# Second block: queries, keys and values ahead of the convolution inputs, and the convolution's taps spread further back

## The reference

```
xn = rms_norm(x, norm1_g)
proj = xn @ w_in + b_in                 # 2048 conv columns, 1024 q, 128 k, 128 v
conv: a * sigmoid(gate), causal depthwise convolution over 31 tokens on 1024 channels,
      + bias, layer_norm over the channels, silu
attention: rms norm of q and k heads, partial rotary, window of 128, sinks, softmax, values
x = x + concat(conv_out, attn_out) @ w_out
x = x + peer(rms_norm(x, norm2_g))      # keys, top-k, 16384 experts computed densely
```

## Time and profile before

| | us |
|---|---|
| median of 3 runs | 3307.56 (3307.48 to 3308.05) |
| the profiled execution's own time | 3305.67 |
| its span, first to last instruction | 3303.9 |
| PE busy | 3249.3 (98%) |
| PEld busy | 2823.9 (85%) |
| DVE busy | 2296.0 (69%) |
| ACT busy | 1546.5 (47%) |
| chain of waits: PE, DVE, ACT | 89%, 9%, 2% |
| mean granted TensorE clock | 0.995 |

### The profile page before, as it was taken

The page is one execution under the profiler, slowest core; times in us unless marked ns, Lnnn a source line. Parts: engine busy times, 40 slices in busy tenths (PEclk is TensorE's granted clock), DMA queues, the critical chain, the costliest instruction groups (busy, mean ns, idle before and its releaser), DMA issues.

```text
span 3303.9 us, 47459 instructions
## 1 busy us (share of the span) xinstructions
PE 3249.3 (98%) x19858; PEld 2823.9 (85%) x19858; DVE 2296.0 (69%) x3281; ACT 1546.5 (47%) x1975; POOL 9.9 (0%) x22
## 2 busy tenths in 40 slices
PE   9999999999999999998999999999999999999999
PEld 7998888888888888887789999888888888888887
DVE  6765556677577577798669987578787577865554
ACT  4554444555455355455544444444343444435353
POOL 0000000000000000000000000000000000000000
PEclk9999999999999999999999999999999999999999
DMA  7546666656655655552455554655656565565665
GB/s 239 162 150 213 216 207 180 210 188 189 190 191 184 198 186 172 185 163 69 158 160 167 170 169 135 196 168 156 183 173 191 186 184 180 182 185 188 192 189 166
DMA packets 163095, 592.25 MB, mean 179 GB/s; under 512 B 18112, under 2 KB 18272, under 8 KB 161984
## 3 DMA queue, kind: packets, MB, share of 16 engines
q1 hardware_dynamic: 161424, 583.15, 56.3%
q0 software_dynamic: 1456, 6.06, 0.6%
HBM read 587.04 MB, written 2.10 MB: 178 GB/s over the span
## 4 chain that ended last, share of the span: by engine, by line
PE 89%; DVE 9%; ACT 2%; issue 1%; DMA 0%; SPq 0%; DVEq 0%; ACTq 0%
PE PS L1063 19%; PE PS L1083 15%; PE PS L1085 14%; PE PS L1084 14%; PE PS L1066 10%; PE PS L1093 4%; PE PS L1094 4%; PE PS L1095 4%; DVE LO L1582 3%; PE PS L1260 1%; DVE GB L1996 1%; PE PS L1273 1%; ACT HI L1282 1%; PE PS L1117 0%; ACT UN L1358 0%
## 5 line engine op out<-in xcount | busy, mean ns | idle before, releaser
L1582 DVE TENSOR_TENSOR LO<-RAW,HI 128x1024 fp32r<-128x1024 f32 x1096 | 1327.0, 1218 | 731.9 <-ACT HI L1282 728.7
L1282 ACT ACTIVATE HI<-RAW 128x1024 fp32r<-128x1024 f32 x1096 | 1149.7, 1054 | 1149.9 <-PE PS L1085 722.1
L1063 PE MATMUL PS<-XX,HI 128*128 128x512 f32 x2688 | 735.5, 395 | 0.0
L1083 PE MATMUL PS<-HI,FH 128*128 128x512 f32 x1760 | 694.4, 395 | 5.7 <-DVE FL L1582 5.4
L1085 PE MATMUL PS<-HI,FL 128*128 128x512 f32 x1760 | 686.8, 390 | 0.0
L1084 PE MATMUL PS<-LO,FH 128*128 128x512 f32 x1760 | 685.3, 389 | 0.0
L1063 PEld LDWEIGHTS PS<-XX,HI 128*128 128x128 f32 x2688 | 459.6, 189 | 61.9
L1093 PE MATMUL PS<-XX,HI 128*128 128x256 f32 x1664 | 479.1, 288 | 9.8 <-DVE LO L1582 9.5
L1094 PE MATMUL PS<-XX,HI 128*128 128x256 f32 x1664 | 471.2, 283 | 0.0
L1095 PE MATMUL PS<-XX,LO 128*128 128x256 f32 x1664 | 471.0, 283 | 0.0
L1066 PEld LDWEIGHTS PS<-XX,LO 128*128 128x128 f32 x2688 | 412.4, 189 | 57.2
(11 more groups left out here) (280 smaller groups left out, 2090.7 us busy)
## 6 DMA issues: line engine op xcount, KB each, us to landing
RAW<-in_peer_v SPq DMA_DIRECT2D x256, 512.0 KB, 4.0
RAW<-in_ffn_w_up SPq DMA_DIRECT2D x176, 512.0 KB, 4.2
RAW<-in_peer_ut_rest SPq DMA_DIRECT2D x160, 512.0 KB, 3.6
RAW<-in_w_in SPq DMA_DIRECT2D x136, 512.0 KB, 4.2
RAW<-in_peer_ut SPq DMA_DIRECT2D x96, 512.0 KB, 3.6
RAW<-in_ffn_w_down SPq DMA_DIRECT2D x88, 512.0 KB, 3.9
RAW<-in_w_mix_out SPq DMA_DIRECT2D x32, 512.0 KB, 3.8
RAW<-in_w_in_2c SPq DMA_DIRECT2D x32, 512.0 KB, 3.6
```

Source lines behind the costliest of these rows:

```text
L1063: e.matmul(o, hi[:, k, x], XX[:, 4 * u + k, :, :].rearrange("p h s -> p (h s)"), start=first and k == 0, stop=False, skip_group_check=True)
L1083: e.matmul(o, x, hi[:, k, :], start=first and k == 0, stop=False, skip_group_check=True)
L1282: return e.activation(dst, src, ACT.Copy) if scale is None else e.activation(dst, src, ACT.Copy, scale=scale)
L1582: return e.tensor_tensor(dst, src, hi.bitcast(F32), ALU.subtract)
```

## The change

The order of the second block's list is rewritten. `q2,0` to `q2,2` come first, with 16 diagonals beside them and no taps. Beside `h2,0` go the heads' norms and 14 empty background advances; attention follows them at rate 1.5, beside `h2,1` to `h2,3`, with two taps for each unit. The loop without weight units now ends when attention and the second set of diagonals are through (its background rate is still 2), and no longer waits for TensorE's conv blocks or the taps. `o2` carries what the taps' generators give, one advance a unit; behind it a loop runs until taps and TensorE's conv blocks are done, and only then `layer_normed` is appended and flushed, before `o2_last`. Blocks 4 and 5 take three taps for each advance. R2 and RD2 move into the first block's mask, and the wait on `h2,3` before the copy of attention's output goes. The weight units' list follows the new order of products. The numbers of instructions on each engine stay the same.

```diff
@@ plan: the order of weight units
-    units("w_in_2c", [0, 1])
     units("w_in_2q", [0, 1])
     units("w_in_2kv", [0], 256)
-    units("w_in_2c", [2, 3])
+    units("w_in_2c", range(4))
@@ plan: the second block
-    conv_input(0)
-    beside.append(causal([0, 1], 3))
-    conv_input(1)
-    beside.append(causal([2, 3], 3))
     background.append(build(range(16)))
     for g in range(3):
         product(("q2", g), 8)
@@
-    beside.insert(0, together(heads_normed(0), heads_normed(1)))
+    beside.append(together(heads_normed(0), heads_normed(1)))
+    background.append(pause(14))
+    background.append(attention(2, (1, 2)))
     background.append(build(range(16, 31)))
-    background.append(attention(2, (1, 2)))
+    rate[0] = 1.5
+    conv_input(0)
+    beside.append(causal([0, 1], 2))
+    conv_input(1)
+    beside.append(causal([2, 3], 2))
     conv_input(2)
-    beside.append(causal([4, 5], 4))
+    beside.append(causal([4, 5], 3))
     conv_input(3)
     on_pe = [causal_pe((6, 7))]
     rate[0] = 2
-    while on_pe or (2, 1) not in done:
+    while background or (2, 1) not in done:
         step()
         advance(on_pe)
-    while beside:
-        advance(beside)
     rate[0] = 1
@@
-    background.append(layer_normed())
     for g in range(4):
         product(("o2", g), 4)
         emit("o2", g)
+    while on_pe or beside:
+        advance(beside)
+        advance(on_pe)
+    background.append(layer_normed())
     flush()
@@ buffers
-    R2, RD2 = STAGE[:, 8, :], STAGE[:, 9, :].rearrange("p (t s) -> p t s", t=2)
+    R2, RD2 = const("mask1")[:, 0:256], const("mask1")[:, 256:512].rearrange("p (t s) -> p t s", t=2)
@@ scalar: att_value
                 if a_ == 2:
                     w.wait_ge(s_mm, multiplied(LAST_DOWN))
-                    w.wait_ge(s_dve, V("h2", 3, k=2))
```

## The result

The changed kernel took 3335.26 us (median of 4 runs, 3334.06 to 3336.43) against 3307.52 (3306.58 to 3308.05) beside it: a ratio of 1.0086, 95% interval 1.0073 to 1.0099. Slower by 27.7 us, where 17.2 were forecast. The time lies above the band that the forecast itself was given (3317 to 3332, with a chance of 0.62) and inside the wider range (3311 to 3338), near its upper end.

The account below looks back on a forecast made before the run. TensorE, busy 98% of the span, was taken to bound the kernel. The steps summed to 292.6 us against 275.2, less 0.2 for a shorter first unit: +17.2 on 3307.56, about 3325 us, range 3311 to 3338.

Parts of the forecast that it names:

- q2: Queries, keys and values first, with diagonals and no taps beside them: bound by TensorE, 52.7 us.
- four conv inputs: Units h2,0 to h2,3 with heads' norm and attention beside them: 108.7 us, bounds 106.2 and 120.
- left before o2: Stretch without weight units ahead of o2, with 10 attention steps and 18 taps: 31.5 us, bounds 23.3 and 36.
- o2: 16 weight units with two taps each, the LayerNorm's matmuls no longer in it: 43.5 us.
- behind o2: Weight units stopped while 88 taps and 27 conv matmuls are left: 36.5 us, bounds 29 to 38.
- LayerNorm, with its share of slow clock: Bare LayerNorm chain between the taps and o2_last: 16.1 us, plus 2.0 for slow mean and variance matmuls.
- slow clock at o2_last: TensorE's reduced clock at o2_last's start, after idleness: 1.6 us.
- Heads' norm and attention beside the conv inputs: Norm beside h2,0: 9.7 us of stalls and slow clock become 0.6; attention beside h2,1 to h2,3: 1.4 of stalls.
- in-order rival: Attention beside conv inputs starves the divisions: 120 us there, 36 before o2, 3341 in all; chance 0.18.
- The charge for the clock: TensorE's slow clock after idleness: 2.0 us at mean and variance matmuls, 1.6 at o2_last's start.
- Cheap by itself: Work standing alone runs at its own rate: attention rest 18.9 us, a tap 0.31, total 3299; chance 0.07.
- The wash: Rest before o2 takes only TensorE's 23.3 us, no stall before it: 3315, or 3311 with cheaper taps; chance 0.13.

Follow-up runs that it names:

- e6_diag: Changed kernel with diagonals 16 to 30 built ahead of attention, which also begins one advance earlier: 3333.15 us, 1.0079 to the kernel before.
- e3_out_last: Changed kernel with VectorE's copy of TensorE's conv block 7 queued behind all taps: 3331.11 us, 1.0077 to the kernel before.
- e2_back: Kernel before with only the back half of the change, the loops around o2 and the bare LayerNorm: 3319.11 us, 1.0040 to the kernel before.
- e4_warm: Changed kernel with idle filler matmuls on TensorE beside the last taps and in the LayerNorm: 3334.28 us, 1.0086 to the kernel before.
- v2_spread: Kernel before, attention two advances later, rate 2 beside h2,3; remaining taps and conv blocks under o2's start, LayerNorm under its last two groups: 3311.94 us, 1.0018.
- v6: Kernel before with one conv input ahead of q2, attention beside the last three; last taps, then LayerNorm under o2: 3307.75 us, 1.0002.
- v7: As v6, but all taps finished before o2 and the LayerNorm beside o2 from its start: 3305.08 us, 0.9995 to the kernel before.
- e5_three: Changed kernel with three taps instead of two for each advance in blocks 0 to 3: 3321.08 us, 1.0046 to the kernel before.

## Why the prediction was right or wrong

Right in sign and mechanism (taps and LayerNorm left bare), too small by 10.5 us: the time missed the forecast's own band of 3317 to 3332 and stayed inside the range because that left room for stalls. By its steps, forecast and measured in us:

| step | forecast | measured |
|---|---|---|
| q2 | 52.7 | 54.0 |
| four conv inputs | 108.7 | 109.2 |
| left before o2 | 31.5 | 36.2 |
| o2 | 43.5 | 43.8 |
| behind o2 | 36.5 | 41.2 |
| LayerNorm, with its share of slow clock | 18.1 | 19.2 |
| slow clock at o2_last | 1.6 | 2.6 |
| sum | 292.6 | 306.2 |

The last row is 0.06 of 43.5 us, from that window's clock of 0.94; by the starts of its first matmuls it is 2.4. The 275.2 of before taken off leaves +31.0; the stretch before was cut 0.4 us short, as o2_last began at 1633.9. The rest of the profile is within a microsecond of what it was, and the difference of spans is 30.2. The medians differ by 27.7. q2's excess of 1.3 was not looked into beyond one wait of 0.8 us for an operand of the spread.

*Heads' norm and attention beside the conv inputs.* Right: no wait of 5 us before the transposes, VectorE at 87%, and 109.2 us where the in-order rival wanted 120.

*What is left before o2: the first step that was mis-sized, by 4.7.* The forecast counted from the list of steps, by which attention has passed the third exp of its second query block when the units end, and so it put one exp and three divisions into the stretch. The engines were behind the list. ScalarE's timeline in the changed kernel, the first part of each of the four exps (each four parts of 0.49 us), the first division and the first diagonals:
```profile
1519.00 0.49 ACT L1360 ACTIVATE UN<-UN,SM 128x256 f32<-128x256 f32 x1
...
1521.92 0.49 ACT L1360 ACTIVATE UN<-UN,SM 128x256 f32<-128x256 f32 x1
...
1524.83 1.69 ACT L1284 ACTIVATE UN<-UN,SM 128x256 f32<-128x256 f32 x4
...
1526.43 0.49 ACT L1360 ACTIVATE UN<-UN,SM 128x256 f32<-128x256 f32 x1
...
1534.10 0.51 ACT L1360 ACTIVATE UN<-UN,SM 128x256 f32<-128x256 f32 x1
...
1541.95 1.27 ACT L1284 ACTIVATE UF<-CONST,PAR 128x128 f32<-128x128 f32 x4
```
When the units ended at 1521.4, one exp was done; three exps and all four divisions lay in the stretch. TensorE waited 5.1 us for the first division, a term that the forecast didn't have, and then 2.9 for h2,3's output, where it had 4: together 4.0 more, most of the 4.7. The diagonals were too dear in the forecast, not too cheap: by the list 8 stand before the last values and not 12. That the backlog makes the excess is read from this trace; e6_diag, which happens to start attention one advance earlier, moves the wait to h2,3's output and saves 1 to 2 us, and no run removes the backlog itself.

*Behind o2: the second, again by 4.7.* The taps were counted right (88 at 0.397 = 34.9), but I gave conv block 7's copy its own 0.4 us and not its wait. I had written that 12 us of conv matmuls go "with" the taps; the copy sits among the taps in an in-order queue. e3_out_last took 4.9 us off the tail, and 3 to 4 off the timed runs, by moving that one instruction.

*LayerNorm and clock.* Right to 1.1 and 1.0 us. e2_back gives the bare LayerNorm its price by itself. The charge for the clock was 3.6. The profile has 1.9 at the mean matmuls, none to speak of at the variance and 2.4 to 2.6 at o2_last, yet e4_warm, which removed the part at o2_last, gained nothing that can be timed; the bound on it is a few microseconds.

*The rivals.* In-order stalls gave 3341 and is nearer in number than my forecast, but not by its place: its 120 us didn't come, only its 36 before o2 did, and the tail's stall, the same mechanism, wasn't in it. Cheap by itself fell on the tap: 0.397 alone, and by the rule of the Trainium skill that the prediction weighed ("VectorE: DVE Perf Modes", on the errata) 60 taps would have ended in 19.6 us, where the trace shows 23.84. It also fell on the attention rest, 36.2 instead of 18.9. The wash needed 23.3 there. The same premise, time in proportion to the steps left, misled me again in v2_spread: 35 attention steps in 64.1 us (the prediction has 34), 29 in 64.6, and v6 and v7 with 21 in 61.1. TensorE is busy for some 46 us of v7's stretch, whatever waits lie between; whether its own work or the last block's chain of waits sets the length wasn't separated.

## What to carry to other kernels

An engine's free time is worth something only beside work that must run anyway: count the slots under the bottleneck's units before and after a reordering, and price what is left over at its full rate (here 24 q2 units lost room for 72 taps, and e5_three's 46 taps put back under units were worth 14 us, some 3 of them by a shorter wait). Don't take the list of steps for the state of the engines: count what is still queued when the units end (here three exps and not one). When work for one engine is moved to where it runs alone, look for each instruction in its queue that waits for another engine: everything behind it is delayed, however independent. A stretch in which many engines wait for each other need not shrink in proportion to the work taken out of it (here from 35 attention steps to 21, and from 64.1 us to 61.1).

## What the runs showed of the hardware that was not expected

TensorE's granted clock was low again after only 3.5 us of idleness: in e4_warm eight mean matmuls took 1.89 us at full clock, and behind those 3.48 us the next eight took 3.34 (0.58). After the changed kernel's 10.3 us of idleness o2_last's first matmuls were 0.43 us apart instead of 0.227 for about 5 us. Around these the Trainium skill ("TensorE: Matmul & The Clock Gate", What's actually happening) has half rate as the default that activity lifts, and both runs agree. What e4_warm won back in its profile (2.5 us of span) was not to be found in its timed runs.
